# Paged sample attention with page rings of its own, and prompt attention with two unit tracks taken alternately

## What is computed

```python
z = jnp.einsum('bqhd,bkhd->bhqk', qi, kf) * scale + bf
mask = k_pos[None, :] < q_pos[:, None]
log_beta = jax.nn.log_sigmoid(z)
log_keep = jnp.where(mask, jax.nn.log_sigmoid(-z), 0.0)
later = lax.cumsum(log_keep, axis=3, reverse=True) - log_keep
w = jnp.where(mask, jnp.exp(log_beta + later), 0.0)
return jnp.einsum('bhqk,bkhd->bqhd', w, vf)
...
k_past = cache_sb_k[ie][page_table].reshape(B, past_len, SB_HEADS, SB_HD)
v_past = cache_sb_v[ie][page_table].reshape(B, past_len, SB_HEADS, SB_HD)
```

## Time and profile before

| | |
|---|---|
| three runs, median (range) | 3366.98 us (3362.43 to 3375.03) |
| profiled execution, its own time | 3365.0 us |
| its span, first to last instruction | 3363.4 us |
| PE busy over the span | 3034.1 us (90%), 18088 instructions |
| DVE, ACT, POOL busy | 1192.5, 973.4, 550.2 us |
| prompt attention block | about 640 to 919 us of the span |
| sample attention block | about 919 to 1112 us |

### The profile page before, as it was taken

How to read it: one execution, slowest core, us unless ns; L and a number is a source line. 1 busy time by engine, 2 the same in 40 slices (tenths; PEclk the granted TensorE clock), 3 DMA queues, 4 the chain that set the end, 5 groups by cost and what they waited for, 6 DMA issues and landing times. The chain is left out here.

```text
span 3363.4 us, 44363 instructions
## 1 busy us (share of the span) xinstructions
PE 3034.1 (90%) x18088; PEld 2696.1 (80%) x18088; DVE 1192.5 (35%) x1924; ACT 973.4 (29%) x1418; POOL 550.2 (16%) x328
## 2 busy tenths in 40 slices
PE   5799999888876797999999999798697999999997
PEld 3788999733343697999999998793597999999997
DVE  4155651266522154222222226304335222222225
ACT  2233342266632232211112213211433112212221
POOL 1211011011112211211212212110121122212220
PEclk7899999899988898999999999898798999999998
DMA  5322223200065421112212114106221111111112
GB/s 224 113 83 89 78 82 100 81 11 1 5 209 163 125 77 50 51 57 69 75 50 68 57 44 135 47 15 154 91 62 59 35 50 50 44 31 50 50 46 99
DMA packets 240220, 250.38 MB, mean 74 GB/s; under 512 B 9203, under 2 KB 196007, under 8 KB 239813
## 3 DMA queue, kind: packets, MB, share of 16 engines
q1 hardware_dynamic: 224949, 216.90, 21.2%
q0 software_dynamic: 5120, 16.78, 1.6%
q10 hardware_dynamic: 10016, 14.80, 1.2%
HBM read 207.82 MB, written 29.99 MB: 71 GB/s over the span
## 5 line engine op out<-in xcount | busy, mean ns | idle before, releaser
L616 PE MATMUL PS<-trunk_x_hi,trunk_w_hi 128*128 128x364 f32 x2208 | 740.6, 335 | 95.0 <-POOL trunk_w_lo L763 37.6
L617 PE MATMUL PS<-trunk_x_lo,trunk_w_hi 128*128 128x364 f32 x2208 | 737.0, 334 | 0.0
L618 PE MATMUL PS<-trunk_x_hi,trunk_w_lo 128*128 128x364 f32 x2208 | 735.3, 333 | 0.0
L771 POOL TENSOR_TENSOR trunk_w_lo<-trunk_w_raw,trunk_w_hi 128x1024 fp32r<-128x1024 f32 x128 | 306.9, 2398 | 1354.2 <-ACT trunk_w_hi L979 1263.8
L616 PE MATMUL PS<-hidden,trunk_w_hi 128*128 128x364 f32 x1536 | 509.7, 332 | 0.0
L616 PEld LDWEIGHTS PS<-trunk_x_hi,trunk_w_hi 128*128 128x128 f32 x2208 | 423.9, 192 | 102.7 <-POOL trunk_w_lo L763 38.6
L617 PE MATMUL PS<-hidden,trunk_w_hi 128*128 128x364 f32 x1536 | 505.1, 329 | 0.0
L618 PE MATMUL PS<-hidden,trunk_w_lo 128*128 128x364 f32 x1536 | 504.8, 329 | 0.0
L617 PEld LDWEIGHTS PS<-trunk_x_lo,trunk_w_hi 128*128 128x128 f32 x2208 | 424.3, 192 | 0.0
L618 PEld LDWEIGHTS PS<-trunk_x_hi,trunk_w_lo 128*128 128x128 f32 x2208 | 423.5, 192 | 0.0
L1236 DVE TENSOR_TENSOR M<-M,PS 128x364 f32<-128x364 f32 x336 | 178.3, 532 | 465.2 <-PE PS L618 465.1
(11 more groups left out here) (368 smaller groups left out, 3479.7 us busy)
## 6 DMA issues: line engine op xcount, KB each, us to landing
trunk_w_raw<-mlp_w SPq DMA_DIRECT2D x128, 512.0 KB, 3.8
rec_ada_w<-ada_w SPq DMA_DIRECT2D x28, 1024.0 KB, 5.1
spare<-cache_sb_k SPq DMA_DIRECT2D x64, 256.0 KB, 3.2
values<-cache_sb_v POOLq DMA_DIRECT2D x64, 256.0 KB, 4.1
rec_w_raw<-even_w_in SPq DMA_DIRECT2D x28, 512.0 KB, 3.8
x_scratch<-x_new ACTq DMA_DIRECT2D x9, 1456.0 KB, 5.9
trunk_ada_w<-ada_w SPq DMA_DIRECT2D x24, 512.0 KB, 3.9
x_new<-x_scratch SPq DMA_DIRECT2D x6, 1456.0 KB, 11.2
```

What stands on the lines that cost most here:

```text
L616: pe.matmul(out, hi, xh, start=first, stop=False)
L617: pe.matmul(out, hi, xl, start=False, stop=False)
L618: return pe.matmul(out, lo, xh, start=False, stop=last)
L771: pool.tensor_tensor(wl[:, u % 4, :], raw[:, u % 2, :], wh[:, u % 4, :].bitcast(F32), ALU.subtract).then_inc(s_lo, 1)
```

## The change

The class `PageRings` gives K and V pages rings of their own, of 12 and 10 pages, in SBUF that neither `spare` nor `values` takes. The page table, the first 12 K pages and the first 10 V pages are fetched on SP within the prompt block, behind the stores of the rows. The other K pages are issued on SP and the other V pages on POOL in the sample block; the page number is now read behind the wait for the ring place. The turned K pages have both halves of their buffer in `spare`.

In the sample block's PE program the weights are turned in step 4g+6 behind two of its turns, the values come in step 4g+7, the outputs are turned in step 4g+8.

In the prompt block the units stand in two tracks. Run (0,0) comes first and alone; then one unit of track 1 and one of track 0 alternate until both are empty. Each track has its own R and its own output bank; R of a unit waits for the exponents of the unit before it on its track, that is two units back.

```diff
+class PageRings:
+    K, V = 12, 10
...
+    def load_k(self, eng, core, i):
+        at = self.k_page(i)
+        page = eng.value_load(self.pages[0:1, at:at + 1], min_val=0, max_val=core.cache_k.shape[1] - 1)
+        eng.dma_start(self.k[:, i % self.K, :], core.cache_k[0, bass.ds(page, 1)].rearrange("a p h d -> p (a h d)"))\
+           .then_inc(self.s_k[i % self.K], 16)
...
-    for p in range(SBH // 2):
-        for g in range(2):
-            for kt in range(4 * g + 3, -1, -1):
-                units.append((p, g, kt, max(0, kt - 4 * g) * P))
+    TRACKS = ([(1, 1), (3, 1), (1, 0), (2, 0)], [(3, 0), (0, 1), (2, 1)])
+    tracks = [[u for r in runs for u in run_units(*r)] for runs in TRACKS]
+    units, track = run_units(0, 0), [0] * 4
+    while any(tracks):
+        for i in (1, 0):
+            if tracks[i]:
+                units.append(tracks[i].pop(0))
+                track.append(i)
...
+    before = lambda n: max((m for m in range(n) if track[m] == track[n]), default=None)
...
-        R = sb("later", [P, 2, 2, 512])
+        R = sb("later", [P, 2, 2, 2, 512])
...
+            sp.wait_ge(rings.s_pt, 16)
+            for i in range(rings.K):
+                rings.load_k(sp, core, i)
+            for i in range(rings.V):
+                rings.load_v(sp, core, i)
             for i in range(KR):
                 sp.wait_ge(s_out[i], 16 * 3)
...
-                            pe.wait_ge(s_R, n)
+                            pe.wait_ge(s_R, before(n) + 1)
...
-                if n >= 1:
-                    dve.wait_ge(s_acc, 2 * (n - 1) + 2)
-                    dve.wait_ge(s_R, n)
+                if m is not None:
+                    dve.wait_ge(s_acc, 2 * m + 2)
+                    dve.wait_ge(s_R, m + 1)
...
-            for i in range(NPAGES):
-                page = pool.value_load(pages[0:1, v_page(i):v_page(i) + 1], min_val=0, max_val=core.cache_k.shape[1] - 1)
-                if i >= VRING:
-                    pool.wait_ge(s_o, i - VRING + 1)
-                pool.dma_start(vp[:, i % VRING, :], core.cache_v[0, bass.ds(page, 1)].rearrange("a p h d -> p (a h d)"))\
-                    .then_inc(s_v[i % VRING], 16)
+            for i in range(VRING, NPAGES):
+                pool.wait_ge(s_o, i - VRING + 1)
+                rings.load_v(pool, core, i)
...
-            for h in range(NH + 4):
+            for h in range(NH + 5):
...
-                    if i == 0 and g >= 0:
-                        if h % 4 == 2:
-                            values(g, 0)
-                        if h % 4 == 3:
-                            turn_outputs(g)
-                    if i == 2 and g >= 0 and h % 4 == 2:
-                        values(g, 1)
-                if h % 4 == 1 and g >= 0:
-                    turn_weights(g)
+                    if i == 0 and g >= 1 and h % 4 == 0:
+                        turn_outputs(g - 1)
+                    if g >= 0 and h % 4 == 2 and i == 1:
+                        turn_weights(g)
+                    if g >= 0 and h % 4 == 3 and i in (0, 2):
+                        values(g, i // 2)
```

More of the change, by code:

```diff
@@ L1369, in _, with __init__, v_ready, k_page @@
             low(1, 2, 1)
-def sb_prompt(nc, core, tag, KV, VT, spare):
-    units = []
-    for p in range(SBH // 2):
-        for g in range(2):
-            for kt in range(4 * g + 3, -1, -1):
-                units.append((p, g, kt, max(0, kt - 4 * g) * P))
+class PageRings:
+    K, V = 12, 10
+    def __init__(self, nc, es, tag):
+        sb, sem = scope(nc, es, tag)
+        self.pages = sb("table", [1, NSEQ * NPG], I32)
+        self.k = sb("k", [P, self.K, HALF])
+        self.v = sb("v", [P, self.V, HALF])
+        self.s_pt = sem("table_in")
+        self.s_k = [sem(f"k_in{i}") for i in range(self.K)]
+        self.s_v = [sem(f"v_in{i}") for i in range(self.V)]
+        self.s_v_pool = [sem(f"v_in_by_pool{i}") for i in range(self.V)]
+    def v_ready(self, eng, i):
+        if i < self.V:
+            eng.wait_ge(self.s_v[i], 16)
+        else:
+            eng.wait_ge(self.s_v_pool[i % self.V], 16 * (i // self.V))
+    def k_page(self, n):
+        return (2 * (n // 16) + n // 2 % 2) * NPG + 2 * (n // 4 % 4) + n % 2
+    def v_page(self, n):
+        return (2 * (n // 16) + n % 2) * NPG + n // 2 % NPG
+    def load_k(self, eng, core, i):
[3 more added lines that the diff above has]
+           .then_inc(self.s_k[i % self.K], 16)
+    def load_v(self, eng, core, i):
+        at = self.v_page(i)
+        page = eng.value_load(self.pages[0:1, at:at + 1], min_val=0, max_val=core.cache_v.shape[1] - 1)
+        eng.dma_start(self.v[:, i % self.V, :], core.cache_v[0, bass.ds(page, 1)].rearrange("a p h d -> p (a h d)"))\
+           .then_inc(self.s_v[i] if i < self.V else self.s_v_pool[i % self.V], 16)
+def sb_prompt(nc, core, tag, KV, VT, spare, rings):
+    def run_units(p, g):
+        return [(p, g, kt, max(0, kt - 4 * g) * P) for kt in range(4 * g + 3, -1, -1)]
+    TRACKS = ([(1, 1), (3, 1), (1, 0), (2, 0)], [(3, 0), (0, 1), (2, 1)])
[6 more added lines that the diff above has]
+                track.append(i)
     NU = len(units)
@@ L1383, in sb_prompt @@
     diag = lambda n: units[n][2] >= 4 * units[n][1]
-    run = lambda n: sum(first(i) for i in range(n + 1)) - 1
+    before = lambda n: max((m for m in range(n) if track[m] == track[n]), default=None)
+    nth = lambda n: sum(track[m] == track[n] for m in range(n))
+    runs_ended = lambda n: sum(last(m) for m in range(n + 1))
     n_diag = lambda n: sum(diag(i) for i in range(n + 1))
@@ L1410, in _ @@
         def _(sp):
+            sp.dma_start(rings.pages[:, :], core.page_table.rearrange("(a b) g -> a (b g)", a=1)).then_inc(rings.s_pt, 16)
             sp.wait_ge(s_vr, 9)
@@ L1444, in exponents @@
                         if hh == 0:
-                            pe.wait_ge(s_R, n)
+                            pe.wait_ge(s_R, before(n) + 1)
                         q = pe.matmul(PS[:, bank(n, hh), c:512], cols(core, "neg_ones").to_broadcast([P, P]),
-                                      R[:, n % 2, hh, c:512], start=False, stop=True, skip_group_check=True)
+                                      R[:, track[n], nth(n) % 2, hh, c:512], start=False, stop=True, skip_group_check=True)
                     q.then_inc(s_acc, 1)
@@ L1454, in outputs @@
                     pe.wait_ge(s_wm, n_diag(n))
-                if first(n) and run(n) >= 2:
-                    pe.wait_ge(s_oc, run(n) - 1)
+                if first(n) and before(n) is not None:
+                    pe.wait_ge(s_oc, runs_ended(before(n)))
                 if n == 0:
@@ L1462, in outputs @@
                     r = 64 * hh
-                    q = pe.matmul(PS[r:r + 64, 6 + run(n) % 2, c:512], VT[:, kt, (2 * p + hh) * 64:(2 * p + hh + 1) * 64],
+                    q = pe.matmul(PS[r:r + 64, 6 + track[n], c:512], VT[:, kt, (2 * p + hh) * 64:(2 * p + hh + 1) * 64],
                                   w[:, n % 2, hh, c:512], start=first(n), stop=last(n), skip_group_check=True)
@@ L1574, in _ @@
                     dve.wait_ge(s_o, n + 1)
-                    dve.tensor_copy(core.M[:, 4 + p, g * 512:(g + 1) * 512], PS[:, 6 + run(n) % 2, :]).then_inc(s_oc, 1)
+                    dve.tensor_copy(core.M[:, 4 + p, g * 512:(g + 1) * 512], PS[:, 6 + track[n], :]).then_inc(s_oc, 1)
         @block.gpsimd
@@ L1591, in _, with sb_sample @@
                     pool.tensor_tensor(x, x, strict, ALU.mult).then_inc(s_wm, 1)
-def sb_sample(nc, core, tag, KV, spare_k, spare_v):
+def sb_sample(nc, core, tag, KV, spare_k, rings):
     W64 = SBH * TQ
-    KRING, VRING = 4, 8
+    KRING, VRING = rings.K, rings.V
     NPAGES = NSEQ * NPG
@@ L1607, in sb_sample @@
         sb, sem = scope(nc, es, tag)
-        kp = spare_k[:, 0:KRING * HALF].rearrange("p (i f) -> p i f", i=KRING)
-        kT = [spare_k[:, KRING * HALF:8 * HALF].rearrange("p (s k t) -> p s k t", s=2, k=4), sb("k_T", [P, 2, 4, 2 * PAGE])]
+        kp, vp, s_k = rings.k, rings.v, rings.s_k
+        kT = [spare_k[:, 4 * i * HALF:4 * (i + 1) * HALF].rearrange("p (s k t) -> p s k t", s=2, k=4) for i in range(2)]
         new_w = spare_k[:, 8 * HALF:8 * HALF + NG * W64]
-        vp = spare_v[:, 0:VRING * HALF].rearrange("p (i f) -> p i f", i=VRING)
-        pages = sb("pages", [1, NPAGES], I32)
         qb = sb("q_blocks", [P, 4, NSEQ, W64])
@@ L1642, in _ @@
         def _(sp):
[L1643 to L1650 removed]
+            for i in range(KRING, NPAGES):
+                sp.wait_ge(s_T, i - KRING + 1)
+                rings.load_k(sp, core, i)
         @block.gpsimd
         def _(pool):
[L1654 to L1660 removed]
+            for i in range(VRING, NPAGES):
+                pool.wait_ge(s_o, i - VRING + 1)
+                rings.load_v(pool, core, i)
         @block.tensor
@@ L2802, in step @@
                 spare = es.enter_context(nc.sbuf_tensor("spare", [P, HT, TP], F32))
-                sb_prompt(nc, core, "sb_prompt", big, values, flat(spare))
```

(4 more changed lines are left out.)

19 lines of the change are left out of this document (7 added, 12 removed).

## The result

The changed kernel takes 3336.53 us (median of 4 runs, 3334.32 to 3338.63), the kernel before beside it 3364.7 us. The ratio is 0.9899, 95% interval 0.9884 to 0.9913: 1.0% faster. Forecast was 3327 us, range 3300 to 3352.

A forecast was written before the change was run, and what follows sets the result against it. PE was taken to wait for each diagonal unit's own chain in the prompt block and one chain per group in the sample block. 3365.0 - 15 (prompt) - 25 (sample) = 3325, plus 2.0 for the median: 3327 us, range 3300 to 3352.

The forecast's parts named there:

- z to weights: Sample block, first piece of a group's chain: 11.95 us plus half the 0.87 us of copies into M, 12.4.
- Weights to values: Sample block, second piece of the chain: 4.76 us plus two more turns of 1.09 together, 5.8.
- Values to the next turn: Sample block, third piece: 15.5 us, -2.32 for fewer V pages issued during the values, +0.6 for the page number, 13.8.
- From there to the next z: Sample block, last piece: two turns and scores, 3.9 us, less half of 1.09 for the output turn, 3.35.
- What limits a pair?: Prompt block, wide unit with diagonal one: larger of two bounds, 9.1 to 10.0 us, 10.8 for full size; four pairs 39.8.
- The diagonal pace: Prompt block: four diagonal units take 18.5 us, 4.6 each; kept for units 4 to 11 (37.0) and the end (13.9).
- (a): Prompt block, first bound on a pair: PE's order of wide and short unit, 6.5 + 4.7 s us for short size s.
- (b): Prompt block, second bound on a pair: the wide run's own loop from exponents through logarithm and softplus to PE, 9.1 us.
- Rival 1: Prompt block: masks on POOL collide with adds on DVE, 1.35 us a pair; prompt +6, total 3349; chance 0.17.
- Rival 2: Prompt block: PE fills up and waits only for its own work; prompt -35, total 3307; chance 0.10.
- Rival 3: Sample block: V is fetched no sooner, 3 x 4.8 = 14 us less gain, total 3341; chance 0.09.
- Rival 4: Prompt block: two loops in series by each engine's fixed order, 13.7 us a pair; +60, total 3387; chance 0.05.

The follow-up runs named there:

- b4: The changed kernel with each page number read ahead of the wait for the ring place, as before the change; 3329.66 us, ratio 0.9894 to the kernel before.
- c1: The changed kernel with old unit order, w masks first on POOL, page number read ahead of the wait, rings of 8 K and 14 V pages; 3294.4 us, ratio 0.9777.
- a2: The kernel before with the two tracks alone, no rings, old sample program; 3370.35 us against 3372.19, ratio 0.9988.
- a4: The kernel before with one swap on POOL, mask of w of unit t-2 ahead of softplus mask of unit t; 3339.19 us against 3372.19, ratio 0.9899.
- a3: The changed kernel with one swap on POOL, mask of w of unit t-2 ahead of softplus mask of unit t; 3322.4 us, ratio 0.9845.

## Why the prediction was right, and which step failed

The time lies 9.5 us above the forecast, inside the range, and is faster as forecast. From the first zb to the last copy into M the two blocks took 438.6 us for 468.6, 30 less, where 40 were forecast; the other parts differ by a few us either way and cancel here.

- **The sample block** was forecast at -25 and gave -26: periods 34.75 for 35.3, -1.5 for -1.7 behind the last, and -2.9 from the prompt's last exponents to the first z, where -3.5 and +0.8 for the prompt's last mask were forecast. Within the period it is in part luck, since the pieces were off by more than their sum. z to weights took 11.3 us on average for 12.4. Weights to values took 4.6 for 5.8 (turning the weights took 1.09 us where the earlier trace rows has 1.97; the last section says more). Values to the next turn took 14.0 for 13.8, what six pages at POOL's spacing give. From there to the next z it was 4.8 for 3.35: the output turn stayed on the path, and the copies into M stood ahead of z in full, 984.37 to 985.27, not by half. b4 bears out the 0.6 us for the page number, c1 that V bounded.
- **The prompt block** was forecast at -15 and gave about -4, of which 3.4 hang on the clock in units 44 to 47 (a2). The step that failed is "What limits a pair?": it listed PE's order and the wide run's own loop, and left out POOL's order. It also said that "each mask has 3.64 us of the wide exponents to hide under"; the trace has a mask of w that starts 5 us after its w (between two diagonal units; in the pairs the outputs waited for POOL six times, 3.9 us in all). The wait was on view: outputs waited for the mask of w for 17.8 us in ten waits before, and I took a row of masks beside adds for its reason. The diagonal pace of 4.6 us a unit, kept in the forecast, held that same wait: units 12 to 16, 18.5 us there, took 16.6 in a4 without it. With the tie removed (a3) units 4 to 11 do better than the 37.0, 33.2, and four pairs come to some 39.5, close to the 39.8. So (a) and (b) were the right bounds of a kernel that was not yet there.
- **Rival 1** had the right engine and the wrong mechanism: POOL bound, by the order of its program and not by collision, which the changed kernel's own masks and adds put at some 3 us at most. Rival 2 fell: PE did not fill up with the tracks; it did with the swap. Rival 3 fell: z stand 34.75 us apart and not 39 or more, though the V waits shrank only from 30.0 to 25.2 us, where some 20 were forecast. (Its price of 4.8 a period was summed too high: 2.3, 1.5 and the other half of the copies come to 4.2.) Rival 4 fell: pairs took 9.2 to 12.3 us, fourteen of sixteen under 11.3, not 13.7. It named the kind of cause (one fixed order per engine, a wait of one unit that holds another) and not the engine.

## What to carry to other kernels

Before a software pipeline is reordered to hide a wait, look on every engine, the least busy one too, at what stands ahead of the instruction that is waited for: POOL was busy for a sixth of the time and its two statements in the wrong order bound the block. An instruction whose input has been ready for 5 us, on an engine that is idle, is a sign of order, not of load. When one part of a change gives less than its sum, run the parts alone: here the tracks were worth little or nothing, and a swap of two statements gave more than they had been meant to give.

## What I had not expected of the hardware

Where a wait of PE became shorter, the clock behind it was higher. Windows of the first group's turned weights, in the kernel before and in the changed one:

```profile
964.60:966.60 2.00, 1.93 (x9) 1.93 (x10) 0.00 (x0) 0.02 (x1) 0.00 (x0) 0.50 0.03 8
```

```profile
961.20:962.30 1.10, 1.09 (x10) 1.09 (x11) 0.00 (x0) 0.93 (x2) 0.00 (x0) 1.00 0.75 153
```

Behind a wait of 4.5 us the granted clock was 0.50, the lower of the two levels (1.2 GHz), and behind one of 1.1 us it was 1.00. The changed kernel has both: its last group's weights, behind the wait of 11.7 us, again took 1.97 us. Between these the same wait can go either way: behind 2.69 us in the prompt block the clock fell to 0.50 in a2 and stayed at 1.00 in the changed kernel. With the swap alone (a4), PE's busy time over units 4 to 47 fell from 194.1 us at 0.98, in the window below, to 189.6 at 1.00, with the same instructions: 4.5 of the 26.7 us that I had not counted.

```profile
686.24:912.60 226.36, 194.06 (x654) 78.97 (x653) 142.98 (x198) 154.59 (x214) 40.17 (x56) 0.98 0.00 1
```
